# Modulation sums gathered as rows of one PSUM bank, with ScalarE scaling the weights in 16 of 20 steps

## The chip, the cores and the metric

The kernel runs on one core of one Trainium2 chip, in one launch. The metric is the time of an execution on the device, in microseconds (us); lower is better. The core has five engines that run side by side and meet at semaphores: TensorE (PE; its weight loads are listed as PEld), VectorE (DVE), ScalarE (ACT), GpSimd (POOL) and SyncE (SP), which issues most of the DMAs.

## The reference, cut to what matters

Two blocks stand one behind the other, for 256 tokens of width 1024, in float32. The first is a feed-forward network (FFN1), a mixer and a second feed-forward network (FFN2). The second block is a mixer and an MLP whose norms are modulated by a vector computed from `c`:

```python
def swiglu_ffn(x, w_in, w_out):
    gate, up = jnp.split(x @ w_in, 2, axis=-1)
    return (jax.nn.silu(gate) * up) @ w_out
...
c_act = jax.nn.silu(c)                    # 1024 values
mod = c_act @ w_ada[l] + b_ada[l]         # w_ada is 1024 x 6144
shift1, scale1, gate1, shift2, scale2, gate2 = jnp.split(mod, 6)
```

The vector `mod` depends on `c` alone, so the kernel computes it in 24 steps of 256 columns beside other work. The 20 first ones are done in FFN1 (steps 0 to 9) and FFN2 (steps 10 to 19), the last 4 in the MLP.

## The kernel before, in words

All large products run on TensorE in three passes of rounded float32 (high by high, high by low, low by high). Weights come in slabs of 128 x 2048 floats (1 MB), through a ring of `SLOTS = 3` slots. Each slab goes through four stations: SP issues its DMA into `raw`; ACT rounds it into `wh` (`cast`, lines 856 and 862) when the DMA has landed and TensorE has taken the slab three before it; DVE subtracts, `wl = raw - wh` (`sub`, lines 1348 and 1353), and counts `low_done`; TensorE multiplies (`wide`, line 2079; `deep`, line 2123) and counts `taken`. SP waits for `low_done` of the slab three before, since that frees `raw`, before it issues a DMA.

An FFN has 11 hidden tiles of 256 (`FF_STEPS`). After a prologue it runs in passes. Pass p of TensorE (`one_pass`, p = 0 to 9, one outside the loop and nine in it) takes three slabs that are named here g(p), u(p) and d(p): the gate's and the up's weights of the next hidden tile, 48 matmuls each with 256 columns, and the down weights of the present one, 48 matmuls. Behind them stand `modulate` (lines 2171 to 2177), and a product with zeros, `long_zeros`, which waits for the gate bank to be read (line 2151 issues it). In the listings the loop bodies of the other engines stand one pass ahead:

- ACT: cast g(p+1), silu of the gate, cast u(p+1), wait until d(p) is taken, round the hidden tile (`round_hidden`, line 895), cast d(p+1).
- DVE: read the gate bank (line 1375), subtract for g(p+1), read the up bank (line 1375), subtract for u(p+1), product of the two halves (`hidden`, line 1411), its low part (line 1415), subtract for d(p+1).
- SP: DMA of g(p+1), of u(p+1), of d(p+1), and the DMA of the modulation's weights for step p+1 (line 547) into the one buffer `ada_raw`.

An engine that waits holds up whatever stands behind the wait in its order.

A step of the modulation before the change: POOL waits for the DMA, multiplies the 128 x 2048 weights by `c_act` (line 692), adds the halves three times (lines 695, 697 and 701: 1024, 512 and 256 columns), the last into `ada_sum`. TensorE turns the sum over the 128 partitions into two columns of bank 7 by two float32 products of `ada_sum` with one column of ones (line 2175). SP issues the next step's DMA when the third addition is done (`ada_free`). 
Of the kernel before, what the change touches and what calls it, by code (L numbers as in the profile page):

```python
# [16 lines left out]
P = 128  # L17
# [139 lines left out]
def slab_plan():  # L157
# [20 lines left out]
    for k in range(1, MLP_STEPS):  # L178
# [20 lines left out]
    "sums": (("n1_stat", 1), ("n2_stat", 1), ("qk_stat", 1), ("short_stat", 1), ("o_stat", 1), ("n3_stat", 1),  # L199
             ("g_stat", 1), ("f_stat", 1), ("lat_stat", 1), ("ln_stat", 1), ("y_stat", 1), ("x3_stat", 1), ("z_stat", 1)),  # L200
    "row_banks": (("gate_row", 2), ("z_bank", 4)),
    "row_reads": (("gate_kept", 2), ("z_sq", 4)),
    "row_steps": (("blocks_inverted", 1), ("mo_half", 1), ("g_add", 3), ("gate_ready", 1), ("z_total", 2)),
    "roots": (("n1_std", 1), ("n2_std", 1), ("qk_std", 1), ("short_std", 1), ("o_std", 1), ("n3_std", 1),
# [81 lines left out]
def two_blocks(nc, a):  # L286
    with ExitStack() as ctx:
# [15 lines left out]
        con = sb("con", [P, CON_FLOATS])  # L303
        raw = sb("raw", [P, SLOTS, SLAB])
        wh = sb("wh", [P, SLOTS, SLAB], F32R)
        wl = sb("wl", [P, SLOTS, SLAB], F32R)
# [140 lines left out]
        y_eps, z_eps, scale_m = kr, kr_raw, ps[6][:, T:2 * T]  # L447

        gate_row, z_rows, z_junk = w_qn[:, 0:D], w_kn, w_v
        upad_out = w_qr.rearrange("p (a n) -> p a n", a=2)  # L450
# [34 lines left out]
        def at(name, count):  # L485

            return S(name), count + SHARED.get(name, (name, 0))[1]
# [35 lines left out]
        def _(sp):  # L523
# [18 lines left out]

            def modulation(step):

                if not isinstance(step, int) or step:
# [136 lines left out]
        def _(pool):  # L682
            ps_ = Steps(pool, s_pstep)
            pool.memset(zero[:, :], 0.0).then_inc(S("zero"), 1)

            pool.memset(qkvp[:, :, 0:3], 0.0).then_inc(S("pads"), 1)
            pool.memset(mpad[:, :, 0:2], 0.0).then_inc(S("pads"), 1)
            def modulation(step):
# [5 lines left out]
                pool.wait_ge(*at("ada_part", step * 3 + 1))  # L694
                pool.tensor_tensor(flat[:, 0:1024], flat[:, 0:1024], flat[:, 1024:2048], ALU.add).then_inc(S("ada_part"), 1)  # L695
                pool.wait_ge(*at("ada_part", step * 3 + 2))
                pool.tensor_tensor(flat[:, 0:512], flat[:, 0:512], flat[:, 512:1024], ALU.add).then_inc(S("ada_part"), 1)  # L697
                pool.wait_ge(*at("ada_part", step * 3 + 3))
                if not isinstance(step, int) or step:
                    pool.wait_ge(*at("ada_taken", step))  # L700
                pool.tensor_tensor(ada_sum[:, :], flat[:, 0:256], flat[:, 256:512], ALU.add).then_inc(S("ada_free"), 1)
# [14 lines left out]
            pool.wait_ge(low_done, 3)  # L716
            modulation(0)
# [65 lines left out]
            pool.memset(upad[:, :, 0:PAD], 0.0).then_inc(S("upads"), 1)  # L783
            with pool.Fori(0, FF_STEPS - 1) as i:
                modulation(i + (FF_STEPS - 1))

            pool.wait_ge(*at("pos_loaded", 16))
            step(pool.tensor_copy(ang, cosines.bitcast(I32)))
# [51 lines left out]
            with pool.Fori(0, ADA_MLP) as i:  # L840
                modulation(i + ADA_EARLY)

# [4 lines left out]
        def _(act):  # L847
# [38 lines left out]
            def ffn(name):  # L886
# [6 lines left out]
                def round_hidden(count, high=fh):  # L893
                    act.wait_ge(*at(name + "_h", count))
                    act.activation(high[:, :, :], pair(hid[:, 3, :]), ACT.Copy).then_inc(S(name + "_fh"), 1)

                cast(s0 + 3)
                silu(1)
                cast(s0 + 4)
                round_hidden(1)  # L900
                with act.Fori(0, FF_STEPS - 2) as i:
                    s = s0 + 2
# [438 lines left out]
        def _(dve):  # L1341
# [35 lines left out]
            def modulation_vectors():  # L1377
# [5 lines left out]
                dve.tensor_tensor(final_sq, vecs("final_norm"), vecs("final_norm"), ALU.mult).then_inc(S("final_sq"), 1)  # L1383
                dve.wait_ge(*at("ada_taken", ADA_EARLY))
                g, r = VECS["b_ada_2"]
                n = 2 * ADA_EARLY
                st(dve.tensor_tensor(ada[:, 0:n], ps[7][:, 0:n], vec[:, g * P + r:g * P + r + n], ALU.add))
                st.sync()
# [100 lines left out]
            s0 = FIRST["mix"]  # L1489
            dve.wait_ge(*at("pads", 2))  # L1490
            dve.wait_ge(*at("con_rest", 16))
# [573 lines left out]
        def _(pe):  # L2065
# [104 lines left out]

            def modulate(step):

# [6 lines left out]
            def square_sums(n):  # L2179
                for b in range(4):  # L2180
                    pe.wait_ge(*at(n + "_add", b + 1))
                    mm = pe.matmul(ps[6][:, 0:T], ones, sq[:, 2 * b, :], start=(b == 0), stop=(b == 3), skip_group_check=True)
                mm.then_inc(S(n + "_stat"), 1)

            def ffn(name, n, high, low, prev_free):
# [6 lines left out]
                if name == "ffn1":  # L2192
# [20 lines left out]
                def one_pass(i, begin=False):  # L2213
# [18 lines left out]
                for m in range(KT):  # L2232
# [439 lines left out]
            with pe.Fori(0, ADA_MLP) as i:  # L2672
                for r in range(SLOTS):
# [54 lines left out]
```

## Time and profile before

| what | us |
|---|---|
| median of 3 runs | 1005.16 (1004.38 to 1011.98) |
| the profiled execution, its own time | 1004.26 |
| its span in the profile | 1002.4 |
| PE busy | 975.8 |
| DVE busy | 779.9 |
| ACT busy | 501.8 |
| POOL busy | 511.0 |

The span runs from the first to the last instruction; the time holds 1.9 us around it. A busy time is the sum of an engine's instructions, and shares of time are not what decides: in each stage it is read which wait ends last. A listed duration of a matmul (278 ns) is longer than its pitch in a row, since matmuls overlap.

### The profile page before, as it was taken

To read this page: it belongs to the slowest core of one execution; us is meant where nothing else is said; L and a number is where in the kernel's file an instruction comes from. 1 tells how busy PE (TensorE), PEld (TensorE's weight loads), DVE (VectorE), ACT (ScalarE), POOL (GpSimd) and SP (SyncE) were. 2 spreads that over 40 slices of the span, in tenths; PEclk is the share of its full clock that TensorE was granted. 3 is DMA by queue.
4 is the path that set the end of the run, shared out by engine and by line. 5 is a ranking of instruction groups with operands and counts; after the bars stand their busy time and mean duration, and the time that the engine had idled before them with its cause. 6 is when DMAs were issued, how large, how long until landed. Compare 5 with 4: busy or idle time off the path is not lost.

```text
span 1002.4 us, 18812 instructions
## 1 busy us (share of the span) xinstructions
PE 975.8 (97%) x7645; PEld 926.8 (92%) x7645; DVE 779.9 (78%) x810; ACT 501.8 (50%) x587; POOL 511.0 (51%) x302
## 2 busy tenths in 40 slices
PE   9999999999989999999999999999989989999997
PEld 8999999998979899999999999978979979999996
DVE  5776565799995679887787779998978887768764
ACT  7433433477541474434334756667657454343432
POOL 4575767610054037577577699999940104314400
PEclk9999999999998999999999999999989999999999
DMA  8966858747360277686776475572236517675641
GB/s 270 360 211 227 275 194 276 242 129 211 96 198 8 84 224 244 232 270 209 261 241 213 140 194 159 142 216 85 85 109 204 193 50 245 228 247 195 216 161 43
DMA packets 166494, 190.06 MB, mean 190 GB/s; under 512 B 10654, under 2 KB 155628, under 8 KB 166316
## 3 DMA queue, kind: packets, MB, share of 16 engines
q1 hardware_dynamic: 165580, 186.13, 57.1%
q0 software_dynamic: 688, 3.07, 1.1%
q8 instruction: 36, 0.59, 0.2%
q10 hardware_dynamic: 176, 0.15, 0.1%
q14 instruction: 14, 0.11, 0.0%
HBM read 187.17 MB, written 2.16 MB: 189 GB/s over the span
## 4 chain that ended last, share of the span: by engine, by line
PE 73%; DVE 15%; POOL 4%; issue 3%; ACT 2%; SPq 1%; DMA 1%; ACTq 0%; DVEq 0%; POOLq 0%
PE ps L2079 46%; PE ps L2123 11%; PE ps L2131 9%; DVE wl L1348 5%; DVE ps L1756 2%; POOL work L825 2%; POOL con L822 2%; PE ps L2364 1%; PE ps L2310 1%; ACT wh L856 1%; PE ps L2175 1%; SPq L564 1%; POOL work L818 1%; PE ps L2151 1%; PE ps L2235 1%
## 5 line engine op out<-in xcount | busy, mean ns | idle before, releaser
L2079 PE MATMUL ps<-xh,wh 128*128 128x256 f32 x1208 | 340.1, 282 | 6.4 <-DVE work L1375 3.2
L2079 PE MATMUL ps<-xl,wh 128*128 128x256 f32 x1208 | 335.4, 278 | 0.0
L2079 PE MATMUL ps<-xh,wl 128*128 128x256 f32 x1208 | 335.2, 278 | 0.0
L1353 DVE TENSOR_TENSOR wl<-raw,wh 128x2048 fp32r<-128x2048 f32 x78 | 231.5, 2968 | 67.4 <-ACT wh L862 67.1
L2079 PEld LDWEIGHTS ps<-xh,wh 128*128 128x128 f32 x1208 | 228.1, 189 | 12.3 <-issue 7.1
L2079 PEld LDWEIGHTS ps<-xl,wh 128*128 128x128 f32 x1208 | 227.8, 189 | 0.5
L2079 PEld LDWEIGHTS ps<-xh,wl 128*128 128x128 f32 x1208 | 227.5, 188 | 0.0
L862 ACT ACTIVATE wh<-raw 128x2048 fp32r<-128x2048 f32 x78 | 149.9, 1922 | 138.3 <-PE ps L2079 101.4
L1348 DVE TENSOR_TENSOR wl<-raw,wh 128x2048 fp32r<-128x2048 f32 (+1 forms) x72 | 181.5, 2527 | 32.7 <-ACT wh L856 32.0
L692 POOL TENSOR_TENSOR ada_raw<-ada_raw,c_act 128x2048 f32<-128x2048 f32 x24 | 90.6, 3775 | 206.5 <-DMA ada_raw<-in_w_ada 201.3
L856 ACT ACTIVATE wh<-raw 128x2048 fp32r<-128x2048 f32 (+1 forms) x74 | 139.5, 1889 | 59.4 <-PE ps L2079 42.3
L2079 PE MATMUL ps<-yh,wh 128*128 128x256 f32 x480 | 135.7, 283 | 1.2 <-DVE work L1884 0.7
L2079 PE MATMUL ps<-yh,wl 128*128 128x256 f32 x480 | 133.6, 278 | 0.0
L2079 PE MATMUL ps<-yl,wh 128*128 128x256 f32 x480 | 133.5, 278 | 0.0
L2079 PEld LDWEIGHTS ps<-yh,wh 128*128 128x128 f32 x480 | 90.8, 189 | 4.3 <-issue 2.0
L2079 PEld LDWEIGHTS ps<-yl,wh 128*128 128x128 f32 x480 | 91.0, 190 | 0.1
L2079 PEld LDWEIGHTS ps<-yh,wl 128*128 128x128 f32 x480 | 90.7, 189 | 0.0
L2123 PE MATMUL ps<-fh,wl 128*128 128x256 f32 x320 | 88.5, 277 | 0.0
L2123 PE MATMUL ps<-fh,wh 128*128 128x256 f32 x320 | 88.5, 276 | 0.0
L2123 PE MATMUL ps<-fl,wh 128*128 128x256 f32 x320 | 88.5, 276 | 0.0
L695 POOL TENSOR_TENSOR ada_raw<-ada_raw 128x1024 f32<-128x1024 f32 x24 | 82.3, 3427 | 1.9
L697 POOL TENSOR_TENSOR ada_raw<-ada_raw 128x512 f32<-128x512 f32 x24 | 72.4, 3016 | 1.9
(426 smaller groups left out, 1773.0 us busy)
## 6 DMA issues: line engine op xcount, KB each, us to landing
raw<-in_ffn_w_in SPq DMA_DIRECT2D x43, 1024.0 KB, 7.6
ada_raw<-in_w_ada SPq DMA_DIRECT2D x24, 1024.0 KB, 5.1
raw<-in_ffn_w_out SPq DMA_DIRECT2D x22, 1024.0 KB, 6.5
raw<-in_w_in SPq DMA_DIRECT2D x18, 1024.0 KB, 5.3
raw<-in_w_mlp_in SPq DMA_DIRECT2D x16, 1024.0 KB, 5.5
raw<-in_w_mlp_out SPq DMA_DIRECT2D x16, 1024.0 KB, 4.9
raw<-in_w_mix_in SPq DMA_DIRECT2D x14, 1024.0 KB, 5.4
raw<-in_w_mix_out SPq DMA_DIRECT2D x4, 1024.0 KB, 5.2
```

Source lines behind the costliest of these rows:

```text
L692: pool.tensor_tensor(ada_raw[:, :, :], ada_raw[:, :, :], c_act[:, :].unsqueeze(2).to_broadcast([P, KT, 256]), ALU.mult).then_inc(S("ada_pa ...
L695: pool.tensor_tensor(flat[:, 0:1024], flat[:, 0:1024], flat[:, 1024:2048], ALU.add).then_inc(S("ada_part"), 1)
L697: pool.tensor_tensor(flat[:, 0:512], flat[:, 0:512], flat[:, 512:1024], ALU.add).then_inc(S("ada_part"), 1)
L822: ins = pool.tensor_scalar(tap_own[:, n, :], upad[:, t, k:k + T], tap(k, t), 0.0, ALU.mult, ALU.add)
L825: ins = pool.tensor_tensor(sums, sums, tap_own, ALU.add)
L856: act.activation(wh[:, s % SLOTS, 0:n], raw[:, s % SLOTS, 0:n], ACT.Copy).then_inc(high_done, 1)
L862: act.activation(wh[:, s % SLOTS, :], raw[:, s % SLOTS, :], ACT.Copy).then_inc(high_done, 1)
L1348: dve.tensor_tensor(wl[:, s % SLOTS, 0:n], raw[:, s % SLOTS, 0:n], wh[:, s % SLOTS, 0:n].bitcast(F32), ALU.subtract).then_inc(low_done, 1)
L1353: dve.tensor_tensor(wl[:, s % SLOTS, :], raw[:, s % SLOTS, :], wh[:, s % SLOTS, :].bitcast(F32), ALU.subtract).then_inc(low_done, 1)
L2079: mm = pe.matmul(bank[:, m * T:(m + 1) * T], w[:, k, m * P:(m + 1) * P], r[:, k, :], start=(m == 0 and k == 0 and j == 0), stop=(k == KT - ...
L2123: mm = pe.matmul(ps[m // 2][:, (m % 2) * T:(m % 2 + 1) * T], w[:, k, m * P:(m + 1) * P], r[:, k, :], start=(begin and k == 0 and j == 0 an ...
L2131: mm = pe.matmul(ps[n][:, :], r[:, k, tk * P:(tk + 1) * P], w[:, k, half * 512:(half + 1) * 512], start=False, stop=stop, skip_group_check ...
```

## The change

- ACT scales. In steps 2 to 9 and 12 to 19 POOL's multiplication by `c_act` is replaced by eight activations of 128 x 256 on ACT (`scale_rows`), in place in `ada_raw`, behind the cast of d(p+1) in ACT's loop, for step p+2 (p+12 in FFN2). Steps 0, 1, 10 and 11 stay on POOL.
- POOL's first addition writes into another buffer (`ada_fold`), so that `ada_raw` is free after it. SP's next DMA waits for that first addition (`ada_part`), no longer for the whole step.
- The sum is split into a high part, rounded by ACT (`high_sum`, which also writes the 20 columns of `step_pick` for this step), and a low part, subtracted by POOL. `high_sum` stands between `round_hidden` and the cast of d(p+1), and waits for POOL's third addition.
- TensorE adds one product in place of two: `step_pick` (128 x 20, one column of ones) by both parts (512 columns), accumulated into 20 rows of bank 7. The product with zeros at the end of each pass goes, and one clears bank 7 in FFN1.
- At the end of FFN2 DVE copies the 20 rows to SBUF, TensorE turns them into columns with four small products inside the last down slab (`turn_rows`), and DVE waits for these.
- Memsets of small pads and of the line of ones are moved on POOL.

The diff's core:

```diff
-                    sp.wait_ge(*at("ada_free", step))
+                elif not isinstance(step, int) or step:
+                    sp.wait_ge(*at("ada_part", step * 5 - 3))
                 sp.dma_start(ada_raw[:, :, :], rows["w_ada_2"][:, :, bass.ds(step * 256, 256)]).then_inc(S("ada_loaded"), 16)
...
-            with pool.Fori(0, FF_STEPS - 2) as i:
-                modulation(i + 1)
+            modulation(1, "ffn1")
+            with pool.Fori(0, FF_STEPS - 3) as i:
+                modulation(i + 2, "ffn1", scale=False)
...
+                def high_sum(step):
+                    if not isinstance(step, int) or step:
+                        act.wait_ge(*at("ada_taken", step))
+                    act.wait_ge(*at("ada_part", step * 5 + 4))
+                    act.activation(step_pick[:, :], step_line[:, bass.ds(step * -1 + (ADA_EARLY - 1), ADA_EARLY)], ACT.Copy)
+                    act.activation(ada_parts[name][:, 0, :], ada_fold[name][:, 0:256], ACT.Copy).then_inc(S("ada_part"), 1)
+
+                def scale_rows(step):
+                    act.wait_ge(*at("ada_loaded", step * 16 + 16))
+                    for k in range(KT):
+                        ins = act.activation(ada_raw[:, k, :], ada_raw[:, k, :], ACT.Copy, scale=c_act[:, k:k + 1])
+                    ins.then_inc(S("ada_part"), 1)
...
                     round_hidden(i + 2)
+                    high_sum(i + (first + 1))
                     cast_in_loop(s + 5, i, 3, 1)
+
+                with act.Fori(0, FF_STEPS - 3) as i:
+                    one_pass(i)
+                    scale_rows(i + (first + 2))
+                one_pass(FF_STEPS - 3)
...
+            def modulate(step, name):
+
+                pe.wait_ge(*at("ada_free", step + 1))
+                pe.matmul(ps[7][0:ADA_EARLY, :], step_pick[:, :], ada_parts[name].rearrange("p a t -> p (a t)"), start=False, stop=False, skip_group_check=True)\
+                    .then_inc(S("ada_taken"), 1)
...
-                    modulate(i + (0 if name == "ffn1" else FF_STEPS - 1))
-                    pe.wait_ge(*at(name + "_gate", i + 2))
-                    long_zeros(gate_bank)
+                    modulate(i + (0 if name == "ffn1" else FF_STEPS - 1), name)
```

ACT's loop in FFN1, before, from its first instruction to the branch (line 862 casts g, u and d in this order, 891 is silu, 895 rounds the hidden tile):

```order
L861 ISA [waits slot2_loaded]
L862 ACTIVATE wh<-raw 128x2048 [waits taken]
L890 REGISTER_ALU
L891 ACTIVATE hid<-hid 128x512 [waits s_hidden_gate]
L860 REGISTER_ALU
L861 REGISTER_ALU [waits slot0_loaded]
L862 ACTIVATE wh<-raw 128x2048 [waits taken]
L907 REGISTER_ALU
L895 ACTIVATE fh<-hid 128x512 [waits s_hidden,taken]
L862 ACTIVATE wh<-raw 128x2048 [waits taken,slot1_loaded]
L901 REGISTER_ALU
L901 COMPARE_AND_BRANCH
```

The same loop after the change, from the rounding of the hidden tile (now line 929) to the branch; line 896 is the cast of d, 935 and 936 are `high_sum`, 941 is `scale_rows`:

```order
L929 ACTIVATE fh<-hid 128x512 [waits s_hidden,taken]
L933 REGISTER_ALU
L934 ISA [waits s_ada_taken]
L935 ISA [waits s_ada_part]
L935 ACTIVATE step_pick<-step_line 128x20
L936 ACTIVATE yl<-work 128x256
L896 ACTIVATE wh<-raw 128x2048 [waits taken,slot1_loaded]
L939 ISA
L941 ACTIVATE ada_raw<-ada_raw,c_act 128x256 [waits s_ada_loaded]
L941 ACTIVATE ada_raw<-ada_raw,c_act 128x256 x7
L962 REGISTER_ALU
L962 COMPARE_AND_BRANCH
```

What moved: ten activations and two waits (for POOL's third addition and for the DMA of the modulation's weights) now stand in ACT's order, two ahead of the cast of d and eight behind it, all of them ahead of the next pass's cast of g.

SP's loop in FFN1 after the change, whole; lines 541 are the DMAs of g and u, 546 that of d, 554 that of the modulation's weights:

```order
L541 ISA [waits low_done]
L541 DMA raw<-in_ffn_w_in 128x8x256
L536 REGISTER_ALU
L541 ISA [waits low_done]
L541 DMA raw<-in_ffn_w_in 128x8x256
L536 REGISTER_ALU
L541 ISA [waits low_done]
L546 DMA raw<-in_ffn_w_out 128x2x1024
L553 ISA
L554 ISA [waits s_ada_part]
L554 DMA ada_raw<-in_w_ada 128x8x256
```

What moved: nothing in the order; only the semaphore of the last wait is another (before it was `s_ada_free`). The DMA of the modulation's weights still stands behind the DMA of d and its wait for `low_done`.

TensorE's end of a pass in the loop, before:

```order
L2123 MATMUL ps<-fh,wl 128x256
L2175 ISA [waits s_ada_free]
L2175 MATMUL ps<-con,ada_sum 128x1
L2175 ISA
L2175 MATMUL ps<-con,ada_sum 128x1
L2222 REGISTER_ALU
L2151 MATMUL ps<-zero 128x512 [waits s_hidden_gate]
L2226 REGISTER_ALU
L2226 COMPARE_AND_BRANCH
```

and after (the line of `deep` is now 2186):

```order
L2186 MATMUL ps<-fh,wl 128x256
L2237 MATMUL ps<-yl,step_pick 20x512 [waits s_ada_free]
L2304 REGISTER_ALU
L2304 COMPARE_AND_BRANCH
L2313 MATMUL ps<-yl,wh 128x256 [waits low_done,s_hidden_low]
```

What moved: two products of `ada_sum` and the product with zeros are replaced by one of 512 columns.

## Rows read from the trace of the kernel before

**Rows 1.** The page's first part: busy time, share of the span, instructions

```profile
PE 975.8 (97%) x7645; PEld 926.8 (92%) x7645; DVE 779.9 (78%) x810; ACT 501.8 (50%) x587; POOL 511.0 (51%) x302
```

**Rows 2.** The chain that ended last, FFN1 and FFN2: start, length, what

```profile
60.49 11.53 PE ps L2079 x96
...
89.43 5.44 PE ps L2123 x48
...
182.87 11.10 PE ps L2079 x96
...
411.48 11.10 PE ps L2079 x96
...
531.84 11.10 PE ps L2079 x96
```

**Rows 3.** Timeline of PE at the end of a pass: start, length, engine, line, what

```profile
77.40 0.28 PE L2123 MATMUL ps<-fh,wl 128*128 128x256 f32 x1
77.52 0.50 PE L2175 MATMUL ps<-con,ada_sum 128*128 128x1 f32 x4
77.95 0.38 PE L2151 MATMUL ps<-zero 1*128 1x512 bf16 x1
78.26 0.39 PE L2079 MATMUL ps<-xh,wh 128*128 128x256 f32 x1
```

**Rows 4.** Timeline of ACT, FFN1 loop and (last row) POOL's tap scaling

```profile
95.14 0.63 ACT L895 ACTIVATE fh<-hid 128x512 fp32r<-128x512 f32 x1 [3.75 <-DVE hid L1411]
95.68 1.91 ACT L862 ACTIVATE wh<-raw 128x2048 fp32r<-128x2048 f32 x1
575.66 1.70 ACT L1097 ACTIVATE ada_raw<-work,vec 128x256 f32<-128x256 f32 x4
```

**Rows 5.** Timeline of SP's issues and of POOL behind them

```profile
65.03 0.37 SPq L541 DMA_DIRECT2D raw<-in_ffn_w_out  x1
77.08 0.37 SPq L547 DMA_DIRECT2D ada_raw<-in_w_ada  x1
402.58 0.37 SPq L541 DMA_DIRECT2D raw<-in_ffn_w_out  x1
403.21 0.37 SPq L547 DMA_DIRECT2D ada_raw<-in_w_ada  x1
410.23 3.61 POOL L692 TENSOR_TENSOR ada_raw<-ada_raw,c_act 128x2048 f32<-128x2048 f32 x1 [7.23 <-DMA ada_raw<-in_w_ada]
```

**Rows 6.** Timeline of DVE and POOL where they overlap, FFN1 (last row: FFN2)

```profile
45.37 3.60 POOL L692 TENSOR_TENSOR ada_raw<-ada_raw,c_act 128x2048 f32<-128x2048 f32 x1 [11.47 <-DMA ada_raw<-in_w_ada]
45.42 5.70 DVE L1353 TENSOR_TENSOR wl<-raw,wh 128x2048 fp32r<-128x2048 f32 x1 [1.13 <-ACT wh L862]
62.55 2.29 DVE L1353 TENSOR_TENSOR wl<-raw,wh 128x2048 fp32r<-128x2048 f32 x1 [1.12 <-ACT wh L862]
82.29 3.66 POOL L692 TENSOR_TENSOR ada_raw<-ada_raw,c_act 128x2048 f32<-128x2048 f32 x1 [5.37 <-DMA ada_raw<-in_w_ada]
86.03 2.41 POOL L695 TENSOR_TENSOR ada_raw<-ada_raw 128x1024 f32<-128x1024 f32 x1
87.28 3.31 DVE L1353 TENSOR_TENSOR wl<-raw,wh 128x2048 fp32r<-128x2048 f32 x1 [2.56 <-ACT wh L862]
91.43 2.48 DVE L1353 TENSOR_TENSOR wl<-raw,wh 128x2048 fp32r<-128x2048 f32 x1 [0.24 <-ACT wh L862]
91.84 2.66 POOL L701 TENSOR_TENSOR ada_sum<-ada_raw 128x256 f32<-128x256 f32 x1
93.83 1.22 DVE L1411 TENSOR_TENSOR hid<-hid 128x512 f32<-128x512 f32 x1
400.33 2.68 POOL L701 TENSOR_TENSOR ada_sum<-ada_raw 128x256 f32<-128x256 f32 x1
```

**Rows 7.** Windows around an idle stretch of PE: busy by engine, clock, DMA

```profile
740.00:743.00 3.00, 2.27 (x8) 1.46 (x8) 2.97 (x5) 0.00 (x0) 0.00 (x0) 0.50 0.16 35
743.00:746.00 3.00, 3.00 (x21) 3.00 (x21) 3.00 (x5) 1.90 (x4) 1.71 (x2) 0.70 0.91 314
```

More of the change, by code:

```diff
@@ L304, in two_blocks @@
         raw = sb("raw", [P, SLOTS, SLAB])
+        step_line = sb("step_line", [P, 2 * ADA_EARLY])
+        step_pick = sb("step_pick", [P, ADA_EARLY], F32R)
         wh = sb("wh", [P, SLOTS, SLAB], F32R)
@@ L541, in deep, with modulation @@
                 sp.dma_start(slot(slot_of, 2), rows[w][:, bass.ds(step * 2, 2), :]).then_inc(slot_loaded[slot_of % SLOTS], 16)
-            def modulation(step):
-                if not isinstance(step, int) or step:
+            def modulation(step, late=False):
+                if late:
                     sp.wait_ge(*at("ada_free", step))
+                elif not isinstance(step, int) or step:
+                    sp.wait_ge(*at("ada_part", step * 5 - 3))
                 sp.dma_start(ada_raw[:, :, :], rows["w_ada_2"][:, :, bass.ds(step * 256, 256)]).then_inc(S("ada_loaded"), 16)
@@ L663, in _ @@
                     deep(s + 1 + i * 6, s + 1, "w_mlp_out_2", i * 3 + r)
-                modulation(i + ADA_EARLY)
+                modulation(i + ADA_EARLY, late=True)
             for k in range(ADA_MLP * SLOTS + 1, MLP_STEPS):
@@ L693, in modulation @@
                                    ALU.mult).then_inc(S("ada_part"), 1)
-                pool.wait_ge(*at("ada_part", step * 3 + 1))
+                pool.wait_ge(*at("ada_part", step * 3 + 1 + 2 * ADA_EARLY))
                 pool.tensor_tensor(flat[:, 0:1024], flat[:, 0:1024], flat[:, 1024:2048], ALU.add).then_inc(S("ada_part"), 1)
-                pool.wait_ge(*at("ada_part", step * 3 + 2))
+                pool.wait_ge(*at("ada_part", step * 3 + 2 + 2 * ADA_EARLY))
                 pool.tensor_tensor(flat[:, 0:512], flat[:, 0:512], flat[:, 512:1024], ALU.add).then_inc(S("ada_part"), 1)
-                pool.wait_ge(*at("ada_part", step * 3 + 3))
-                if not isinstance(step, int) or step:
-                    pool.wait_ge(*at("ada_taken", step))
+                pool.wait_ge(*at("ada_part", step * 3 + 3 + 2 * ADA_EARLY))
+                pool.wait_ge(*at("ada_taken", step))
                 pool.tensor_tensor(ada_sum[:, :], flat[:, 0:256], flat[:, 256:512], ALU.add).then_inc(S("ada_free"), 1)
@@ L716, in _ @@
             pool.wait_ge(low_done, 3)
-            modulation(0)
+            modulation(0, "ffn1")
             pool.dma_start(con[:, N_CONST_FIRST:N_CONST], a["table"][:, N_CONST_FIRST:]).then_inc(S("con_rest"), 16)
@@ L783, in _ @@
             pool.memset(upad[:, :, 0:PAD], 0.0).then_inc(S("upads"), 1)
-            with pool.Fori(0, FF_STEPS - 1) as i:
-                modulation(i + (FF_STEPS - 1))
+            for i in range(2):
+                modulation(i + (FF_STEPS - 1), "ffn2")
+            with pool.Fori(0, FF_STEPS - 3) as i:
+                modulation(i + (FF_STEPS + 1), "ffn2", scale=False)
+            pool.wait_ge(*at("ada_free", ADA_EARLY))
             pool.wait_ge(*at("pos_loaded", 16))
@@ L840, in _ @@
             with pool.Fori(0, ADA_MLP) as i:
-                modulation(i + ADA_EARLY)
+                modulation_late(i + ADA_EARLY)
         @block.scalar
@@ L900, in ffn, with one_pass @@
                 round_hidden(1)
-                with act.Fori(0, FF_STEPS - 2) as i:
+                high_sum(first)
+                def one_pass(i):
                     s = s0 + 2
@@ L2183, in square_sums, with turn_rows @@
                 mm.then_inc(S(n + "_stat"), 1)
+            def turn_rows():
+                pe.wait_ge(*at("ada_rows", 1))
+                for half in range(2):
+                    for part in range(2):
+                        mm = pe.matmul(ps[7][:, half * ADA_EARLY:(half + 1) * ADA_EARLY],
+                                       ada_rows[:, part * T + half * P:part * T + (half + 1) * P], ident[0:ADA_EARLY, 0:ADA_EARLY],
+                                       start=(half == 0 and part == 0), stop=(part == 1), skip_group_check=True)
+                mm.then_inc(S("ada_cols"), 1)
             def ffn(name, n, high, low, prev_free):
@@ L2238, in ffn @@
                         mm.then_inc(S(name + "_bank"), 1)
+                    if name == "ffn2" and m == 3:
+                        turn_rows()
                 mm.then_inc(taken, 1)
```

48 lines of the change are left out of this document (40 added, 8 removed).

## The prediction

> **What bounds the kernel now.** I read the page's busy times first, then the chain that ended last, then the timelines of each engine over one pass of an FFN. TensorE is busy for 97% of the span and ScalarE for 50% [rows 1], so in these stages work on ScalarE looks free. The chain says the same of the two loops: it is TensorE's products, pass after pass. From pass 2 (slab g(2), at 60.49) to pass 9 (g(9), at 182.87) FFN1 takes 122.38 us for 7 passes, 17.48 each; FFN2 takes 531.84 - 411.48 = 120.36, 17.19 each [rows 2]. Of a pass 11.1 + 5.44 = 16.54 are its 144 large matmuls [rows 2]. The rest is its end: from the last product of `deep` (77.40) to the next pass's first (78.26) lie 0.86, of which 0.12 is a usual pitch [rows 3].
>
> The busy shares don't tell in which order the stations of a slab depend on each other, and that decides here. SP issues the DMA of a slab d at once when DVE has the low part of the slab d before: low part from 62.55 to 64.84, issue at 65.03 [rows 5, 6]. The modulation's DMA stands behind it in SP's order.
>
> **The change part by part.**
>
> *TensorE.* Per pass two products and the one with zeros go, one of 512 columns comes. The one with zeros has as many columns and holds the next product back by 0.31 (77.95 to 78.26) [rows 3]. I take 0.35 for the new one with the loop's branch, against 0.74 before: some 0.4 less per pass, 20 times. Bounds: 0 and 0.6. It counts only where TensorE is what ends last.
>
> *POOL.* A 3.6 us multiplication goes from 16 steps [rows 5], a subtraction of 256 columns comes (about 0.7). POOL is on the chain in neither loop, so by itself this is worth nothing beyond FFN1's passes getting as short as FFN2's.
>
> *ScalarE, cost of its work.* Four activations of 128 x 256 with a scale from SBUF take 1.70 [rows 4], a pitch of 0.4, so eight take 3.3. `high_sum` is two short ones; by the same pitch and one of 20 columns I take 0.6. If each took its full 0.5 alone, the eight would take 4.0. As busy time that fits: some 7 + 3.9 of 17.
>
> *ScalarE, its wait.* This is the term that decides. In iteration i of its loop ScalarE casts d(i+1) and then waits for the weights of step i+2. Who issues their DMA? SP, in its next iteration, behind the DMA of d(i+2), and that waits for the low part of d(i+1), the very slab just cast. So the load cannot be under way when ScalarE comes to wait for it: it is only asked for after cast, subtraction and SP's issue. Behind the wait stand the scaling and then the cast of g(i+2), which TensorE needs next, and the DVE queue behind that. The looser wait on `ada_part` in SP's code doesn't help, as SP isn't held there but one place earlier.
>
> I follow one turn of this ring, with S the end of the scaling:
> 1. Cast of g: 1.9, to S + 1.9 [rows 4].
> 2. Low part of g on DVE. POOL's first addition starts at S too and takes 2.4 [rows 6]; DVE's subtraction doesn't run beside it. The trace shows that: a subtraction that takes 2.29 alone took 5.70 when issued 0.05 after POOL's 3.60, and 3.31 at 87.28 behind an addition that ended at 88.44 [rows 6]. So it starts at S + 2.45 and ends 2.15 later, S + 4.6.
> 3. Up bank read (0.6), then the low part of u, which first waits for POOL's second addition (1.2 by halving the first): to S + 8.0. Before, the same one took 2.48 [rows 6].
> 4. `hidden`, behind POOL's third addition: 1.22 before [rows 6], to S + 9.2.
> 5. Rounding and `high_sum`: 0.65 + 0.6, to S + 10.45 [rows 4]. POOL's third addition (done at S + 8.6) is not late here.
> 6. Cast of d 1.9, its low part 2.3: S + 14.7 [rows 4, 6]. SP issues d 0.2 later: S + 14.9.
> 7. Modulation weights behind d. Where the trace has the two issues together, d at 402.58 and the weights at 403.21, POOL starts on the weights at 410.23, 7.65 after the first issue [rows 5]. So they are there at S + 22.5.
> 8. Scaling 3.3: the next S is 25.8 to 25.9 after the last.
>
> So a pass takes 25.9, not 17.48 or 17.19; TensorE idles for about 9 of it. There are 8 such scalings per FFN, so 7 full turns between the first and the last g slab that they delay:
> - FFN1: 7 x (25.9 - 17.48) = 58.9. FFN2: 7 x (25.9 - 17.19) = 61.0.
> - First turn, FFN1: step 1 is scaled on POOL, from 45.37 to 48.97 [rows 6]; additions of 2.4, 1.2 and 0.6 and the gaps end at 53.7, as DVE is idle then. `high_sum` of step 1 waits for that, with the cast of d(1) behind it: low part done at 58.5, d(2) issued at 58.7, weights at 66.35, S = 69.7, low part of g(2) at 74.3. TensorE started on it at 60.49 [rows 2]: 13.8 later.
> - First turn, FFN2: the third addition starts at 400.33 and needs 0.6 [rows 6], `high_sum` to 401.6, d(1) cast and subtracted at 405.8, its successor issued at 406.0; then 7.65 + 3.3 + 4.6 give 421.5, against 411.48 [rows 2]: 10.1 later.
> - `turn_rows` and DVE's copy and wait at the end of FFN2: four small float32 products, by the pitch of the old pair (0.43 for two, 77.52 to 77.95 [rows 3]) 0.9, and DVE reads its banks later by about that: 1.5, bounds 0.5 and 3.
> - TensorE's clock. After an idle stretch of some microseconds the granted clock was 0.50, the 1.2 GHz level, in 740 to 743, and 0.70 as a mean over the next 3 us [rows 7]. At about 1 to 2 us a pass this vanishes in the 9 us of idleness, but not in pass 9, where work goes on without a wait: 1.2 in each FFN, 2.4.
> - Pass ends outside the ring, shorter by 0.5 in each FFN: -1.
>
> Sum: 58.9 + 61.0 + 13.8 + 10.1 + 1.5 + 2.4 - 1 = 146.7. On the profiled execution's 1004.26 that is 1151; this execution lies 0.9 below the median of the runs shown. I say 1151.
>
> *Two rules weighed.* The Trainium skill (SBUF — State Buffer, Who interferes with whom) says that VectorE's two-input operations and GpSimd share a port pair as a lock held for the whole instruction. By that rule the trace agrees, as in the 5.70. Without such a lock items 2 to 4 would end 1.45 sooner, the turn would be 24.4 and the sum 21 smaller, some 1130. The skill (TensorE: Matmul & The Clock Gate, HAM oscillation) also warns that a kernel that waits in every tile starts each tile at half clock. The row at 0.50 agrees; the ring has more idle time than that costs.
>
> **Bounds.** Item 7 is the widest. Weights issued alone at 77.08 were used at 82.29, 5.2 later [rows 5, 6]; with the 0.6 of SP's issue a turn could be 1.85 shorter. In the loaded prologue they came 10.5 after their issue (the wait of 11.47 that ends at 45.37 [rows 6] is of that size). But in the ring the queue has been idle for some microseconds when d is issued, as at 402.58, so at most 1 more. Scaling +0.7, the lock -1.45 at most. Turns between 23.5 and 27.7 give, with 14 turns and 2 first ones, -37 to +28: 1114 to 1179.
>
> **The rivals.**
> - *The scaling hides.* If the weights were there when ScalarE comes to them, its 11 us of work fit into 17, the load would start earlier than before, and TensorE's passes would be 16.54 + 0.35 = 16.9. Then 7 x 0.58 + 7 x 0.29 = 6.1 and about 1 of the outer passes are gained, 1.5 given back in `turn_rows`: 1004.3 - 5.6 = 999, no longer slower but 0.6% faster, or 994 if every bound falls well. For it: the shares [rows 1] and the spare time in front of ScalarE's casts. Against it: SP's order. It decides if the load is issued before the cast of d ends. 6%, half of it beyond 1%.
> - *The ring is open.* If the rounding waited only for TensorE's d and not for DVE's queue (items 2 to 4), the turn would start at the end of `deep`: 1.3 for rounding and `high_sum`, 4.3 for d, 0.2, 7.65, 3.3 and 4.6 make 21.4. Then 7 x 3.9 + 7 x 4.2 + 24 = 81, a time of 1085. For it: the rounding did wait for TensorE in passes that ran at full pace. Against it: DVE takes the up bank only behind the low part of g. 4%.
> - *TensorE at half clock throughout.* Were the clock at the 1.2 GHz level for whole passes, 144 matmuls would take 33 and be the bound: 14 x (33.5 - 25.9) = 106 more, 1257. Against it: the clock's mean is 0.70 already in the second window of three microseconds [rows 7]. 3%.
>
> **How the numbers follow.** Forecast 87%, the three rivals 6, 4 and 3. About 1% is what a measurement can tell from no change. Faster by more 3%, within it 3%, slower 94%. The range is the forecast's own, 1114 to 1179; what lies outside are the rivals and the extreme corners of the bounds.
>
> **What would show it.** In the changed kernel's profile ScalarE's first activation of `scale_rows` would wait for the DMA of the modulation's weights, 10 us 8 times per FFN, 160 in all (2.3 + 0.2 + 7.65 behind each cast), TensorE's first product on g would wait for DVE's low part some 9 us in 16 passes, the chain would pass through ScalarE, DVE and DMA in both FFNs, and g slabs would stand 25.9 apart. SP's issue of the weights would stand 0.6 behind that of d. The mixers and the MLP would be as long as before. The prediction is wrong if the weights' DMA is issued before d's cast is over, if that wait is short, or if passes are 17 long.

## The result and the profile after

| what | before, us | after, us |
|---|---|---|
| median of 4 runs each | 1005.18 (1004.38 to 1011.98) | 1155.41 (1151.13 to 1158.5) |
| the profiled execution | 1004.26 | 1151.13 |
| its span | 1002.4 | 1149.2 |

The ratio of the times is 1.1477, with a 95% interval of 1.1424 to 1.153: the change makes the kernel slower by about 15%. The spans differ by 146.8 us.

The page of the kernel after, to be held beside [rows 1]; its last two lines are the granted clock in 40 slices and the chain's shares by engine:

```profile
span 1149.2 us, 18834 instructions
PE 1009.5 (88%) x7574; PEld 958.5 (83%) x7574; DVE 750.9 (65%) x811; ACT 557.9 (49%) x755; POOL 463.5 (40%) x308
...
PEclk9978888779999999978778889999999999999999
...
PE 37%; DVE 20%; DMA 13%; ACT 12%; issue 10%; POOL 5%; SPq 2%; ACTq 1%; DVEq 0%; POOLq 0%
```

ScalarE has 56 us more work and is still idle for half of the span; by shares no engine is the bound. TensorE's granted clock dips in the slices of the two FFNs. Who waits there is in the list of waits (engine, line, what it waited for: us in total, times, the longest):

```profile
DVE wl L1409 <- ACT wh L896: 262.7, 52, 12.8
POOL work L708 <- ACT ada_raw L941: 234.7, 16, 14.8
ACT ada_raw L941 <- DMA ada_raw<-in_w_ada: 166.1, 16, 10.6
...
PE ps L2142 <- DVE wl L1409: 104.7, 16, 10.0
```

Read from the bottom, this is one path: TensorE waits for DVE 16 times, DVE for ScalarE's casts (52 times, as there are several casts in a pass), ScalarE for the modulation's weights 16 times. What makes it a ring is seen in the chain that ended last, here one turn of it in FFN1 (start, length, what). In [rows 2] the same chain was TensorE's alone:

```profile
61.23 7.29 DMA ada_raw<-in_w_ada
...
69.38 2.46 ACT ada_raw L941 x6
71.84 1.81 ACT wh L896
73.67 0.05 DVE wl L1409
...
76.33 0.68 DVE hid L1431
...
79.62 1.23 DVE hid L1474
...
81.46 0.20 ACT step_pick L935
...
81.98 1.82 ACT wh L896
83.82 2.30 DVE wl L1409
...
86.30 0.37 SPq L546
...
86.95 7.37 DMA ada_raw<-in_w_ada
94.35 0.06 ACT ada_raw L941
```

The DMA that ends at 94.32 was issued at 86.95, behind that of d at 86.30, and that one waited for ScalarE's cast at 81.98 and DVE's subtraction. ScalarE stood at its wait from 83.8 on. From one weights' DMA to the next are 25.7 us; the mean of the 14 full turns is 25.6.

The timeline of POOL, DVE and ScalarE in the same turn (start, length, engine, line, what, idle time before), to be held beside [rows 4, 6]:

```profile
71.91 2.35 POOL L708 TENSOR_TENSOR work<-ada_raw 128x1024 f32<-128x1024 f32 x1 [14.85 <-ACT ada_raw L941]
73.67 2.74 DVE L1409 TENSOR_TENSOR wl<-raw,wh 128x2048 fp32r<-128x2048 f32 x1 [12.68 <-ACT wh L896]
81.88 1.91 ACT L896 ACTIVATE wh<-raw 128x2048 fp32r<-128x2048 f32 x1
94.35 3.30 ACT L941 ACTIVATE ada_raw<-ada_raw,c_act 128x256 f32<-128x256 f32 x8 [10.56 <-DMA ada_raw<-in_w_ada]
```

The end of the ring lies in pass 9. The chain there, in FFN1 and in FFN2, with the last down slab (L2313) and the start of the next mixer's products (L2142 at 708.36):

```profile
240.74 7.22 DMA ada_raw<-in_w_ada
...
255.92 14.01 PE ps L2142 x96
269.93 5.44 PE ps L2186 x48
275.37 0.23 PE ps L2237
275.60 5.45 PE ps L2313 x48
...
674.11 13.17 PE ps L2142 x96
687.28 5.44 PE ps L2186 x48
...
695.68 1.01 PE ps L2259 x8
```

And the windows behind the wait that ended at 255.92, and of one whole turn (length; busy time of PE, PEld, DVE, ACT, POOL; granted clock; DMA share; GB/s), beside [rows 7]:

```profile
255.90:258.90 3.00, 2.98 (x14) 2.98 (x15) 3.00 (x2) 0.00 (x0) 2.92 (x2) 0.50 0.65 188
258.90:261.90 3.00, 3.00 (x16) 3.00 (x16) 2.08 (x3) 1.52 (x4) 1.23 (x2) 0.50 0.91 279
76.41:102.22 25.81, 18.98 (x145) 18.57 (x145) 10.75 (x8) 10.28 (x15) 9.04 (x5) 0.83 0.49 163
```

### The profile page after: what moved, and what is told of

It reads as the page before. It is cut to its first block, busy times and chain, and to the rows that moved or that the text cites. A ratio compares the mean times of both kernels' runs of the same rounds, so it can differ in the third digit from the quotient of the medians.

```text
span 1149.2 us, 18834 instructions
## 1 busy us (share of the span) xinstructions
PE 1009.5 (88%) x7574; PEld 958.5 (83%) x7574; DVE 750.9 (65%) x811; ACT 557.9 (49%) x755; POOL 463.5 (40%) x308
## 4 chain that ended last, share of the span: by engine, by line
PE 37%; DVE 20%; DMA 13%; ACT 12%; issue 10%; POOL 5%; SPq 2%; ACTq 1%; DVEq 0%; POOLq 0%
PE ps L2142 23%; DMA ada_raw<-in_w_ada 12%; PE ps L2194 8%; DVE wl L1404 5%; ACT wh L896 5%; DVE wl L1409 4%; ACT ada_raw L941 4%; DVE ps L1819 2%; POOL work L859 2%; DVE hid L1474 1%; POOL con L856 1%; ACT wh L890 1%; PE ps L2186 1%; DVE hid L1431 1%; PE ps L2444 1%
## 5 line engine op out<-in xcount | busy, mean ns | idle before, releaser
L2142 PE MATMUL ps<-xh,wh 128*128 128x256 f32 x1208 | 349.7, 289 | 58.4 <-DVE wl L1409 52.2
L1409 DVE TENSOR_TENSOR wl<-raw,wh 128x2048 fp32r<-128x2048 f32 x78 | 207.0, 2654 | 262.8 <-ACT wh L896 262.7
L2142 PE MATMUL ps<-xl,wh 128*128 128x256 f32 x1208 | 344.5, 285 | 0.0
L2142 PE MATMUL ps<-xh,wl 128*128 128x256 f32 x1208 | 344.0, 285 | 0.0
L2142 PEld LDWEIGHTS ps<-xh,wh 128*128 128x128 f32 x1208 | 237.2, 196 | 65.8 <-DVE wl L1409 55.5
L2142 PEld LDWEIGHTS ps<-xl,wh 128*128 128x128 f32 x1208 | 237.3, 196 | 0.5
L2142 PEld LDWEIGHTS ps<-xh,wl 128*128 128x128 f32 x1208 | 237.1, 196 | 0.0
L2142 PE MATMUL ps<-yh,wh 128*128 128x256 f32 x480 | 145.8, 304 | 54.6 <-DVE wl L1409 52.5
L2142 PEld LDWEIGHTS ps<-yh,wh 128*128 128x128 f32 x480 | 100.7, 210 | 58.7 <-DVE wl L1409 55.8
L708 POOL TENSOR_TENSOR work<-ada_raw 128x1024 f32<-128x1024 f32 x20 | 49.4, 2470 | 235.1 <-ACT ada_raw L941 234.7
L2142 PE MATMUL ps<-yl,wh 128*128 128x256 f32 x480 | 142.8, 298 | 0.0
L2142 PE MATMUL ps<-yh,wl 128*128 128x256 f32 x480 | 142.5, 297 | 0.0
L941 ACT ACTIVATE ada_raw<-ada_raw,c_act 128x256 f32<-128x256 f32 x128 | 52.8, 495 | 166.1 <-DMA ada_raw<-in_w_ada 166.1
L2142 PEld LDWEIGHTS ps<-yl,wh 128*128 128x128 f32 x480 | 100.7, 210 | 0.2
L2142 PEld LDWEIGHTS ps<-yh,wl 128*128 128x128 f32 x480 | 100.2, 209 | 0.0
L2186 PEld LDWEIGHTS ps<-fh,wh 128*128 128x128 f32 x320 | 61.0, 191 | 6.9 <-DVE wl L1409 6.9
```

What stands on the lines that cost most here:

```text
L708: pool.tensor_tensor(fold[:, :], flat[:, 0:1024], flat[:, 1024:2048], ALU.add).then_inc(S("ada_part"), 1)
L941: ins = act.activation(ada_raw[:, k, :], ada_raw[:, k, :], ACT.Copy, scale=c_act[:, k:k + 1])
L1409: dve.tensor_tensor(wl[:, s % SLOTS, :], raw[:, s % SLOTS, :], wh[:, s % SLOTS, :].bitcast(F32), ALU.subtract).then_inc(low_done, 1)
L2142: mm = pe.matmul(bank[:, m * T:(m + 1) * T], w[:, k, m * P:(m + 1) * P], r[:, k, :], start=(m == 0 and k == 0 and j == 0), stop=(k == KT - ...
L2186: mm = pe.matmul(ps[m // 2][:, (m % 2) * T:(m % 2 + 1) * T], w[:, k, m * P:(m + 1) * P], r[:, k, :], start=(begin and k == 0 and j == 0 an ...
```

## The experiments

The theory: SP's order closes a ring (cast of d, low part of d, issue of d's DMA, DMA of weights, scaling, cast of g), and every station between adds its length to each of 14 full turns. The rivals put the loss on ScalarE's work itself, or on TensorE's clock. In the diffs "-" and "+" stand against the changed kernel, "..." for lines left out.

The texts on record name the runs in another order: experiments 1 to 4 are e1 to e4, 5 is e10, 6 is e9, 7 is e8, 8 is e5, 9 is e6, 10 is e7, and 11 and 12 keep their numbers. Experiments 2 to 7 have one run each. Repeated runs of one kernel lie up to 8 us apart here (the ten of experiment 9), so their totals are good to some us, and what they show of a turn is read from their traces.

**1. The weights' DMA moved ahead of u's wait, in SP's loop.**

```diff
 wide(s + i * 3, s, w_in, i * 256 + 256 * start)
+modulation(i + (1 if name == "ffn1" else FF_STEPS))
 wide(s + 1 + i * 3, s + 1, w_in, i * 256 + (D_FF + 256 * start))
 deep(s + 2 + i * 3, s + 2, w_out, i + (start - 1))
-modulation(i + (1 if name == "ffn1" else FF_STEPS))
```

> Only SP's order changes: the modulation's weights are issued between the slabs g and u of an iteration, no longer behind d. Ring theory: the load no longer depends on the slab d that ScalarE has just cast; the ring is now scaling, low part of g (S + 4.6), issue, 7.65, scaling 3.3 = 15.8, shorter than TensorE's pass of 16.9, so passes are about 17 and ScalarE's waits for the weights nearly vanish. What remains is the wait of step 1's high_sum for POOL in each FFN (some 6 in FFN1, little in FFN2): 1006 us, 998 to 1015. Rival A (ScalarE's extra work itself, or the lock between DVE and POOL, makes the passes long): the same work is done at the same places, so the time stays above 1130 and passes above 24. Rival B (a slower clock of TensorE is a cause and not an effect): the granted clock stays near 0.93.

Measured: 996.09 (992.62 to 996.8, 4 runs) against 1006.24 before, ratio 0.9892 (0.9846 to 0.9937). One line moved takes away 159 us, with all of ScalarE's added work in place. The wait for the weights, then the chain over a pass, then the weights' issue and the scaling behind it:

```profile
ACT ada_raw L941 <- DMA ada_raw<-in_w_ada: 14.1, 14, 1.1
```

```profile
63.87 10.89 PE ps L2142 x96
74.76 5.44 PE ps L2186 x48
...
80.44 10.89 PE ps L2142 x96
```

```profile
79.11 0.37 SPq L554 DMA_DIRECT2D ada_raw<-in_w_ada  x1
86.71 3.31 ACT L941 ACTIVATE ada_raw<-ada_raw,c_act 128x256 f32<-128x256 f32 x8 [1.04 <-DMA ada_raw<-in_w_ada]
```

The wait falls from 166 to 14 us, and the passes are TensorE's alone, 16.57 each. Both rivals fall: passes are far below 24, and the mean granted clock is 0.99, not 0.93, so the slow clock was an effect of the waits. The time lies below the range that I gave (998 to 1015). A pass was 0.3 shorter than the 16.9 that I took, in 17 or 18 passes, and the stall that I expected at the first step's sum was a wait of 2.0, not 6; the 48 products behind that wait took 7.29 in place of 5.44.

**2. The weights between u and d** (the same line, one place later).

> Only SP's order changes: the weights are issued between u and d. Ring theory: the ring is now scaling, low part of u on DVE (S + 8.0), SP 0.2, u and weights together 7.65, scaling 3.3 = 19.2, still above TensorE's 16.9: passes of 19.2 us, 6.5 shorter than the 25.7 measured in the changed kernel, 16 times: about 1050 us (1035 to 1065), g slabs 19.2 apart. Rival (any place ahead of d frees the load, TensorE bounds again): 1006. Rival A (work or lock): above 1130.

Measured: 1047.28 (one run). The timeline of two scalings:

```profile
114.89 3.31 ACT L941 ACTIVATE ada_raw<-ada_raw,c_act 128x256 f32<-128x256 f32 x8 [4.18 <-DMA ada_raw<-in_w_ada]
134.51 3.31 ACT L941 ACTIVATE ada_raw<-ada_raw,c_act 128x256 f32<-128x256 f32 x8 [4.27 <-DMA ada_raw<-in_w_ada]
```

A ring without the part from the cast of d on turns in 19.6 us, and the wait is 4.2 to 4.3. The time follows the place in SP's order, in steps: 996, 1047, 1155.

**3. Half of the scaling.** In `scale_rows`, `range(4)` for `range(KT)`. In 16 steps half of the weights stay unscaled, so the kernel leaves out a part of the result.

> The changed kernel with four activations in place of eight in scale_rows; half of the modulation's weights stay unscaled in 16 steps, so four activations of 0.4 each are left out per step. Ring theory: ScalarE's scaling lies inside the ring, so each turn is shorter by 1.6: passes of 24.1, 16 x 1.6 = 26 less, 1129 us. Rival (the scaling is hidden, only the wait counts): the wait for the weights grows by as much as the work shrinks, time 1155, passes 25.7.

Measured: 1126.95. The timeline of two scalings:

```profile
140.49 1.71 ACT L941 ACTIVATE ada_raw<-ada_raw,c_act 128x256 f32<-128x256 f32 x4 [10.53 <-DMA ada_raw<-in_w_ada]
164.69 1.71 ACT L941 ACTIVATE ada_raw<-ada_raw,c_act 128x256 f32<-128x256 f32 x4 [10.53 <-DMA ada_raw<-in_w_ada]
```

The turn is 24.2 here and 24.1 in the mean, 1.5 shorter by the four activations that went (1.6), and the wait in front of them is the same. The scaling's length counts whole, once per turn, while the wait is made elsewhere.

**4. No scaling on ScalarE; POOL does all 20 steps.**

```diff
...
-            modulation(1, "ffn1")
-            with pool.Fori(0, FF_STEPS - 3) as i:
-                modulation(i + 2, "ffn1", scale=False)
+            with pool.Fori(0, FF_STEPS - 2) as i:
+                modulation(i + 1, "ffn1")
...
-                with act.Fori(0, FF_STEPS - 3) as i:
+                with act.Fori(0, FF_STEPS - 2) as i:
                     one_pass(i)
-                    scale_rows(i + (first + 2))
-                one_pass(FF_STEPS - 3)
```

POOL's loop in FFN2 changes in the same way.

> One part of the change undone: POOL scales all 20 steps, ScalarE has no scale_rows; high_sum, the rows and the one product of TensorE stay, SP's order stays. Ring theory: a second ring stays behind, since high_sum waits for POOL's third addition and stands ahead of the cast of d: cast of d 1.9, low part 2.3, SP 0.2, d and weights 7.65, POOL's 3.6 + 2.4 + 1.3 + 0.75 alone (8.1; up to 12 beside DVE), high_sum 0.3 to 0.6: 20.7 to 24.7 a pass, against 17.3 before: 1004 + 15 x 3.4 to 7.4 = 1055 to 1115, middle 1080; ScalarE's wait before step_pick long in each pass. Rival (the scaling on ScalarE is the whole loss): 999 to 1005 and passes of 17.

Measured: 1080.37. ScalarE's `high_sum` in two successive turns:

```profile
119.57 0.22 ACT L932 ACTIVATE step_pick<-step_line 128x20 fp32r x1 [8.98 <-POOL work L712]
141.18 0.22 ACT L932 ACTIVATE step_pick<-step_line 128x20 fp32r x1 [7.78 <-POOL work L712]
```

The ring is closed without `scale_rows` too: the cast of d stands behind `high_sum`, which waits for POOL's sums of weights that were issued behind the d before. It turns in 21.6 here and 21.7 in the mean. Taking the scaling away gives back 75 us of the 150, and the gather alone still costs 75. These are not shares that add up: with the scaling kept and `high_sum` out of the ring (experiment 5), 131 of the 150 stay. The two rings share most of their stations, and the longer one hides the other.

**5. High sum behind the cast of d, in the ring.** In ACT's `one_pass`, `high_sum(...)` and `cast_in_loop(s + 5, i, 3, 1)` swapped.

> The changed kernel with high_sum behind the cast of d, the ring closed. high_sum (0.3 from its start to the cast's start, by the changed kernel's trace) leaves the part of the ring between rounding and the cast of d: turns of 25.4; the first turn of each FFN no longer waits for POOL with d(1) (11.2 and 4.2 in the changed kernel), but the weights of step 2 still come behind d(1): about 16 x 0.3 + 10 + 4 = 19 less, 1136 us (1130 to 1146). Rival (high_sum's wait is what makes each turn long): passes of 17 to 20, under 1070.

Measured: 1136.9. The scalings start at 112.30, 137.63 and 162.83 and wait 10.0 each. Over the 14 full turns a turn is 25.3 instead of 25.6, so the swap is worth the 0.3 that I took, 4 us in all. More came from the first turns, where the sum of step 1 no longer holds the cast of d(1) up: the first scaling starts 6.8 earlier in FFN1 and another 3.7 are gained up to the first one of FFN2. That makes 14 us between the two traces, and 18 between the times. The rival, passes of 17 to 20, fell.

**6. The two issues swapped, behind the same wait.** In SP's loop `free(s + 2 + i * 3)`, then `modulation(...)`, then `deep(...)`.

> The changed kernel with SP issuing the modulation's weights directly ahead of d instead of behind it, after the same wait for the low part of the last d. The ring stays closed, only its DMA term changes. Alone in the queue such a load was used 5.2 after its issue, as second of the pair 7.65 after the first's. Ring theory: each turn is shorter by 2.4: 23.3 a pass, 16 x 2.4 = 39 less, 1117 us. Rival (both loads share the DMA engines whichever is issued first): 1150 and 25.7.

Measured: 1108.65. The chain's DMAs of two turns:

```profile
103.40 5.22 DMA ada_raw<-in_w_ada
126.50 5.24 DMA ada_raw<-in_w_ada
```

First of the pair, the weights land 5.2 after their issue; as the second, 7.2 to 7.4 (240.74 and 86.95 above). The turn is 23.1, 2.5 less where I took 2.4, and 35 us of the gain are in the 14 full turns. The rest lies in the first turns (the first scaling of FFN1 starts 6.1 earlier). The total of 46.7 us between the times is 8 more than the 39 that I gave; between the two profiled executions it is 42.5. The later start of d's load held nothing up: in the loop no cast waits for the DMA of d.

**7. POOL's second and third addition 8 columns wide.** The kernel leaves out most of the modulation's sum.

> The changed kernel with its ring, but POOL's second and third additions work on 8 columns only; most of the modulation's sum is left out. If the lock between DVE and POOL is in the ring as I priced it, DVE's low part of u no longer waits for the second addition (0.65) and hidden not for the third (0.55): turns of 24.5, 16 x 1.2 = 19 less, 1136 us. Rival (POOL is off the ring and its additions cost nothing): 1155 and turns of 25.7.

Measured: 1139.86. The chain's DMAs of the weights start at 83.58, 108.23 and 132.87, so the turn is 24.65, and 24.7 in the mean. So 0.9 a turn, 13 us of the 15.5, is what these additions cost where they lie beside DVE's subtraction of u and the product of the two halves. I had taken 1.2 a turn.

**8. Without the ring, high sum late** (experiment 1 with the swap of 5).

> The version of e1 (weights issued between g and u) with high_sum moved behind the cast of d in ScalarE's loop. In e1 the one stall left is in FFN1's pass 1: TensorE waits 2.0 for d(1), whose cast stands behind high_sum's wait for POOL, and the 48 products behind it take 7.29 in place of 5.44. Theory: both go, 3.9 less, passes stay at 16.57: 992 us (989 to 994). Rival (high_sum is not what holds d(1), or TensorE waits for the modulation's sum instead at the pass's end): 996, and a wait of TensorE for POOL's subtraction appears.

Measured: 994.78 (992.72 to 997.81, 4 runs), ratio 0.9873 (0.983 to 0.9917). By the times this can't be told apart from experiment 1 (996.09), and the 992 that I gave was not reached in the median. The trace shows the wait of 2.0 for d(1) gone and one of 1.7 for the next g in its place, so that the products of g(2) start at 63.18 instead of 63.87. In the profiled execution of experiment 12, the same kernel, that wait is 0.3 and they start at 61.59. So the swap gains 0.7 to 2.3 here, too little for the spread of the times.

**9. Without the ring, POOL scales all** (experiment 4 with SP's order of 1).

> POOL scales all 20 steps (as in e4) and the weights are issued between g and u (as in e1); high_sum and the rows stay. Theory: neither ring closes inside one pass; the weights of step i+2 land some 3 us into a pass, POOL's 8 to 12 end before high_sum is due at the next pass's start, so passes are 16.6 as in e1 and the time is e1's, 996 (992 to 1000): ScalarE's scaling in itself gains nothing. Rival (POOL's four operations don't fit, ScalarE's scaling is needed for the gain): passes of 17.4 or more as before the change and 1003 to 1010.

Measured: 1005.51 (10 runs), ratio 0.9999 (0.9973 to 1.0026). I was wrong. The time is the one that the rival gave, but its reason, that ScalarE's scaling is needed, falls with experiment 10. Three lines of the timeline and one of the waits show what happens:

```profile
403.25 3.60 POOL L703 TENSOR_TENSOR ada_raw<-ada_raw,c_act 128x2048 f32<-128x2048 f32 x1 [0.96 <-DMA ada_raw<-in_w_ada]
403.31 5.70 DVE L1404 TENSOR_TENSOR wl<-raw,wh 128x2048 fp32r<-128x2048 f32 x1 [1.65 <-ACT wh L893]
437.95 4.93 DVE L1404 TENSOR_TENSOR wl<-raw,wh 128x2048 fp32r<-128x2048 f32 x1 [1.65 <-ACT wh L893]
...
PE ps L2181 <- DVE wl L1404: 5.8, 4, 2.6
```

ScalarE does not wait for POOL's sum here (once in the whole kernel, 1.7); it is POOL that waits for ScalarE. `high_sum` stands directly ahead of the cast of d. When it is done, POOL subtracts the low part and goes on to the next multiplication, which starts at 403.25, while ScalarE casts d. DVE's subtraction for d is ready 0.06 later, at 403.31, and takes 5.7, or 4.9 in another pass, instead of 2.3. TensorE waits for d in four passes. Most passes are 16.57 all the same. The loss sits in a few, above all in one of each FFN, where the 48 products behind the wait run at a lower clock (7.34 in place of 5.44 at 76.60).

**10. The same with high sum late.** Now POOL is released only behind the cast of d.

> e6 with high_sum behind the cast of d. Theory: a late sum can then delay only itself, so this is equal to e5, 992 (988 to 996). Rival (ScalarE's scaling is worth something): 3 or more slower than e5.

Measured: 992.88 (989.56 to 994.69, 4 runs), ratio 0.9856 (0.9807 to 0.9906). Two of its passes, and DVE's subtraction for d beside POOL's subtraction and multiplication:

```profile
77.83 10.89 PE ps L2137 x96
...
94.40 10.89 PE ps L2137 x96
...
406.67 2.29 DVE L1404 TENSOR_TENSOR wl<-raw,wh 128x2048 fp32r<-128x2048 f32 x1 [0.86 <-ACT wh L893]
407.15 2.41 POOL L714 TENSOR_TENSOR xh<-work,xh 128x256 fp32r<-128x256 f32 x1 [0.74 <-ACT xh L933]
409.53 5.70 POOL L703 TENSOR_TENSOR ada_raw<-ada_raw,c_act 128x2048 f32<-128x2048 f32 x1
```

DVE starts first, and its subtraction takes 2.29. Now POOL pays, with 2.41 in place of 0.8 and 5.70 in place of 3.60. The passes are 16.57. POOL is busy for 15.59 of such a pass, and nobody waits for it. Which of the two starts first decides which one is held, and POOL's delay costs nothing here.

**11 and 12. Both again, in five rounds on one chip**, for what ScalarE's scaling is worth once SP's order and `high_sum` are mended.

> The kernel of e7 again, to know its time better: 992.9, between 990 and 995, faster than the kernel before by 1.2 to 1.4%.

> The kernel of e5 again beside e11 on one chip: if ScalarE's scaling is worth nothing once the sum is late, the medians lie within 0.3% of each other, about 993 to 995; if it is worth something, this one is below e11 by 3 or more.

Measured: POOL scaling 994.46 (992.68 to 997.63, 6 runs), ratio 0.9879 (0.9848 to 0.991); ScalarE scaling 996.74 (992.98 to 998.66, 6 runs), ratio 0.99 (0.9867 to 0.9933). The medians are 0.23% apart, less than the intervals, and in experiments 8 and 10 POOL's version was ahead too: no gain from ScalarE's scaling is seen. The version of experiment 10 is faster than both kernels, by 1.2 to 1.4% against the kernel before; both intervals exclude 1.

## Why the prediction was right, point by point

The mechanism came as forecast, and the size too. That the predicted 1151 is the profiled execution's 1151.13 to a tenth is luck; against the median of 1155.41 it is 0.4% low, and the medians differ by 150.2. The terms, each measured as the difference of the same product's start in the two traces (g(2) in FFN1: 76.46 against 60.49, FFN2: 494.89 against 411.48):

| term | predicted | measured |
|---|---|---|
| first turn, FFN1 | 13.8 | 16.0 |
| 7 turns, FFN1 | 58.9 | 57.1 |
| pass 9, FFN1 (clock, pass end) | 0.7 | 2.5 |
| mixer of block 1 | 0 | -2.8 |
| first turn, FFN2 | 10.1 | 10.7 |
| 7 turns, FFN2 | 61.0 | 58.9 |
| pass 9, FFN2, with `turn_rows` | 2.2 | 4.2 |
| rest, with rounding | 0 | 0.2 |
| sum | 146.7 | 146.8 |

The sum is closer than its terms deserve: misses of about 2 on both sides cancel, and the mixer's -2.8 differs between executions of one kernel (below). Without it the terms give 149.6.

- *The ring.* Shown: it is on the chain, and moving one SP line opens it (experiment 1). Item by item with S = 71.84, the low part of g ends at S + 4.6 (predicted 4.6), u's at 7.9 (8.0), `hidden` at 9.0 (9.2), `high_sum` at 10.1 (10.45), SP issues d at 14.5 (14.9) and the weights are there at 22.5 (22.5). The mean turn was 25.6, not 25.9.
- *Item 7, the weights behind d.* Right in size: 7.4 + 0.65 = 8.0 against 7.65. The item ended at 22.5 as forecast because item 6 ended 0.4 early. That the DMA of d ahead of it is worth 2 is shown by experiment 6.
- *The lock.* Right: DVE's subtraction for g starts at 73.67 beside POOL's addition and takes 2.74, 0.45 more than alone. Experiment 7 shows 0.9 a turn for the later additions; together that is 1.35 of the 1.45 that the prediction gave the lock. Experiments 9 and 10 show that whichever of the two starts first holds the other up. The Trainium skill (SBUF — State Buffer, Who interferes with whom) says the same, an exclusive lock in which the order of issue decides who blocks, and the trace agrees (5.70 for DVE in one, 5.70 for POOL in the other).
- *First turn, FFN1.* 2.2 too small: step 1's weights were multiplied at 47.36, not at 45.37 [rows 6], and `high_sum` waited until 55.74. Their DMA was not issued later (34.60); it took 12.7 to land, where the prediction's row has 10.5. Why was not looked into.
- *Clock.* In proportion the term that was mis-sized most: 1.2 per FFN predicted, 2.9 and 2.1 measured (14.01 and 13.17 against 11.1 for g and u). The 1.2 was already half of what its own rows give: 3 us at 0.50 and 3 us at 0.70 [rows 7] lose 1.5 + 0.9 = 2.4. Here the granted clock was 0.50 in both windows behind 255.90, and 0.50 and then 0.78 in the two behind 674.10. In the ring itself the slow products cost nothing, as TensorE waits anyway: over a turn it is busy for 18.98 instead of 16.57 and waits 6.5 in the mean, not the 9 that the prediction names as a sign. The Trainium skill (TensorE: Matmul & The Clock Gate, HAM oscillation) describes a kernel whose every tile starts at half clock after its wait, and the trace agrees with the 0.50 at the start of a turn.
- *Pass end, `turn_rows`.* The branch with the new product cost less than I took: 0.23 on the chain between the last product of `deep` and the next pass, and 10.89 for g and u in place of 11.10 (experiment 1), so 16.57 and not 16.9. The products of `turn_rows` took 1.01. With DVE's part and its later reads they cost more than the 1.5: what pass 9 of FFN2 lost beyond the clock is 4.2 - 2.1 = 2.1, and 1.5 - 0.5 = 1.0 was predicted.
- *The mixer's -2.8.* Not predicted: TensorE's stretch from L2364 at 299.24 took 16.1 us before, to 315.34, and the same one after (L2444) 13.2, from 374.75 to 387.99; its first 32 products took 5.40 and 3.76. It need not be the change's doing: the granted clock over the 32 products was 0.67 before and 1.00 after, and the one kernel of experiments 8 and 12 shows both in its two profiled executions (5.42 at 0.67, and 3.76 at 1.00). The difference is one between executions.
- *Rivals.* That the scaling hides fell with the first wait of 10.5. It is what experiment 1 makes of the kernel: 996 against the 999 that I gave it. The open ring needed a rounding that waits for TensorE; it waited for DVE, 4.97 in front of 80.92. Half clock throughout fell too: it is 0.83 over a turn.
- *The range.* Its low end was a turn of 23.5, which doesn't follow from the two bounds named for it: 1.85 and 1.45 off 25.9 give 22.6. With 25.6 measured nothing hangs on it.

Not foreseen in the prediction is what experiment 4 shows: the wait for POOL's sum in `high_sum` closes a ring of its own, hidden behind the longer one.

## What to carry to other kernels

A wait that is added to an engine is to be followed backwards through every in-order queue: if the DMA that it waits for is issued behind something that the same engine must do first, the loop pays the whole round trip each time, whatever the busy shares say. In such a ring all work on the path counts in full, a scaling of 1.6 as well as a lock of 0.9, and an earlier place for one issue is worth more than all of it. Two rings that share stations hide each other: what one part of a change costs alone is not its share of the whole. Once the loop was bound by TensorE again, relieving POOL was worth nothing that could be measured. What is left of the gain fits the shorter end of TensorE's pass, 16.57 instead of 17.19 to 17.48, though that part wasn't run by itself. And a stretch of one trace is held against another execution of the same kernel before a difference of 2 or 3 us in it is explained.

## What was unexpected of the hardware

- After a wait of 6.2 us TensorE's granted clock stayed at 0.50, the 1.2 GHz level, for the 6 us of work from 255.90 to 261.90. After waits of 8.5 and 5.4 us (ended at 76.46 and 674.11) it was 0.50 for 3 us and 0.72 and 0.78 in the next 3. So the loss did not grow with the wait.
- A 1 MB load landed 5.2 us after its issue when it was the first of a pair on SP's queue, and 7.2 to 7.4 when another of 1 MB had been issued 0.65 before it (experiment 6).
- The same kernel ran the same 32 products of the mixer in 5.42 us in one execution and in 3.76 in another, at granted clocks of 0.67 and 1.00.
- The product of 512 columns with 20 columns of weights took 0.23 us on the chain, less than the 0.31 by which the one with zeros had held back what followed [rows 3].
